# Modulation vectors summed by one matmul after a trip through DRAM

## The reference

```python
c_act = jax.nn.silu(c)                       # c: 1 x 1024
mod = c_act @ ada_w[i] + ada_b[i]            # ada_w[i]: 1024 x 9*1024
sh1, sc1, g1, sh2, sc2, g2, sh3, sc3, g3 = jnp.split(mod, 9, axis=-1)
h = modulate(rms_norm(x, ln_ffn1[i]), sh1, sc1)
x = x + 0.5 * g1[:, None, :] * swiglu(h, ffn1_wg[i], ffn1_wu[i], ffn1_wd[i])
h = modulate(rms_norm(x, ln_mix[i]), sh2, sc2)
...
```

## Time and profile before

| | |
|---|---|
| device time, median of 3 runs | 1738.8 us (1735.62 to 1738.81) |
| span of the profiled execution | 1734.1 us (its own device time is not given) |
| TensorE (PE) busy | 1708.0 us, 98% |
| VectorE (DVE) busy | 1412.9 us, 81% |
| ScalarE (ACT) busy | 908.4 us, 52% |
| POOL busy | 435.0 us, 25% |
| DMA | 411.45 MB, mean 237 GB/s; up to 363 GB/s in F0 |
| steps that add tiles into the accumulator (L2927) | 420, 315.3 us of VectorE |
| loads of modulation tiles by POOL (L2163) | 448 of 256 KB |

### The profile page before, as it was taken

How to read it: one execution, slowest core, us unless ns; L and a number is a source line. 1 busy time by engine, 2 the same in 40 slices (tenths; PEclk the granted TensorE clock), 3 DMA queues, 4 the chain that set the end, 5 groups by cost and what they waited for, 6 DMA issues and landing times. The chain is left out here.

```text
span 1734.1 us, 36503 instructions
## 1 busy us (share of the span) xinstructions
PE 1708.0 (98%) x14039; PEld 1667.7 (96%) x14039; DVE 1412.9 (81%) x1924; ACT 908.4 (52%) x1274; POOL 435.0 (25%) x685
## 2 busy tenths in 40 slices
PE   7999999999999999999999999999999999999998
PEld 5999999999999999999999999999999998799998
DVE  6877898788778977898987799779988896788655
ACT  3443367764335533365634356667444567764444
POOL 6322321012223122321232224540322232401000
PEclk9999999999999999999999999999999999999999
DMA  9998858549887787867698865334988772257550
GB/s 338 356 359 279 294 178 280 166 158 321 304 304 242 276 302 270 302 212 272 229 314 305 302 199 191 115 132 156 322 297 293 230 199 83 78 199 251 184 176 25
DMA packets 261793, 411.45 MB, mean 237 GB/s; under 512 B 21950, under 2 KB 204414, under 8 KB 261560
## 3 DMA queue, kind: packets, MB, share of 16 engines
q1 hardware_dynamic: 224968, 290.67, 51.0%
q0 software_dynamic: 36720, 119.36, 19.4%
HBM read 408.90 MB, written 2.63 MB: 237 GB/s over the span
## 5 line engine op out<-in xcount | busy, mean ns | idle before, releaser
L2891 DVE TENSOR_TENSOR lo<-raw,hi 128x2048 fp32r<-128x2048 f32 (+2 forms) x251 | 565.6, 2256 | 162.4 <-ACT hi L2719 161.8
L2719 ACT CAST hi<-raw 128x2048 fp32r<-128x2048 f32 (+2 forms) x266 | 497.4, 1872 | 377.6 <-PE dacc L2388 189.4
L2386 PE MATMUL up<-operand_hi,hi 128*128 128x256 f32 x1952 | 553.1, 283 | 1.4 <-DVE lo L2891 1.4
L2387 PE MATMUL up<-operand_lo,hi 128*128 128x256 f32 x1952 | 552.3, 283 | 0.0
L2388 PE MATMUL up<-operand_hi,lo 128*128 128x256 f32 x1952 | 552.3, 283 | 0.0
L2163 POOL DMA_DIRECT2D ada<-in_ada_w_dram x448 | 267.3, 613 | 841.8 <-DVE ada_acc L2927 793.5
L2386 PEld LDWEIGHTS up<-operand_hi,hi 128*128 128x128 f32 x1952 | 374.4, 192 | 2.3 <-DVE lo L2891 2.0
L2388 PEld LDWEIGHTS up<-operand_hi,lo 128*128 128x128 f32 x1952 | 374.5, 192 | 0.0
L2387 PEld LDWEIGHTS up<-operand_lo,hi 128*128 128x128 f32 x1952 | 374.5, 192 | 0.0
L2927 DVE SCALAR_TENSOR_TENSOR ada_acc<-ada,c_col,ada_acc 128x512 f32<-128x512 f32 x420 | 315.3, 751 | 13.8 <-DMA ada<-in_ada_w_dram 0.6
L2386 PE MATMUL dacc<-act_hi,hi 128*128 128x256 f32 x976 | 276.2, 283 | 0.7 <-DVE act_lo L3103 0.7
(11 more groups left out here) (483 smaller groups left out, 2858.2 us busy)
## 6 DMA issues: line engine op xcount, KB each, us to landing
ada<-in_ada_w_dram POOLq DMA_DIRECT2D x448, 256.0 KB, 4.8
raw<-in_ffn_wg_dram SPq DMA_DIRECT2D x88, 512.0 KB, 5.4
raw<-in_ffn_wu_dram SPq DMA_DIRECT2D x88, 512.0 KB, 5.2
raw<-in_ffn_wd_dram SPq DMA_DIRECT2D x88, 512.0 KB, 5.6
raw<-in_ffn_w_up_dram SPq DMA_DIRECT2D x88, 512.0 KB, 4.6
raw<-in_ffn_w_down_dram SPq DMA_DIRECT2D x46, 512.0 KB, 4.6
raw<-in_hg_w_in_dram SPq DMA_DIRECT2D x32, 512.0 KB, 4.8
raw<-in_attn_w_qkv_dram SPq DMA_DIRECT2D x24, 512.0 KB, 7.7
```

What stands on the lines that cost most here:

```text
L2386: pe.matmul(o, stat[0], mov[0], start=start, stop=False, skip_group_check=True)
L2387: pe.matmul(o, stat[0], mov[1], start=False, stop=False, skip_group_check=True)
L2719: last = act.copy(put(slab(hi, s, SPL)), take(slab(raw, s, RAW)))
L2891: last = dve.tensor_tensor(put(slab(lo, s, SPL)), take(slab(raw, s, RAW)), put(slab(hi, s, SPL)).bitcast(F32), ALU.subtract)
```

## The change

For v = 2 to 29, with v = 0 and 1 as they were:

- A tile is loaded in one DMA of 512 KB, rows on partitions, and the accumulator is 128 x 1024. VectorE adds a tile in one step instead of two; `c_col` has 16 further columns with `c_act` laid 128 to a column, for which SP loads `c` twice more in another layout at the start. A constant `block_ones` (128 x 8) is made by one reduction.
- POOL writes the finished accumulator to `fold_dram` in DRAM (`fold_start`), in 1024 runs of 128 elements (512 bytes), so that row 16a + r of the DRAM tensor holds the output columns of block a from the eight partitions 8r to 8r + 7, one behind the other; it waits for that, and reads the tensor back as 128 x 1024 (`fold_rest`). VectorE adds the eight partial sums of each row and column in one reduction to `folded`, 128 x 128 (`fold_sum`), and PE sums over partitions with one matmul of `folded` with `block_ones`.
- PE's sums stand later: in the loops behind the columns of iteration 4 instead of 3. Those at the ends of F0, F1, F2, F3, C0 and G go into the next phase (`left_vector`); those of A and C1 stay where they are or move into the last `down`. `mod_vector` moves with them, PE's waits for the vectors too, and G's sum waits for the fourth gelu.
- POOL's loop over four vectors is unrolled, with the two fold steps after the fourth load of the next vector. In other phases `fold_start` is ahead of `pre_add` and `fold_rest` behind it. In H and N, POOL waits for the fold's sum before it builds masks and tables, whose place the fold is read into.

```diff
         def tile_steps(m):
 
-            return AG * (m if m < 2 * KB else m - PE_TILES)
+            return AG * m if m < 2 * KB else AG * (2 * KB - PE_TILES) + m - 2 * KB
...
             source = ada_source(v, k) if source is None else source
+            if v >= 2:
+                eng.dma_start(ada_place(m), source).then_inc(full, 16)
+                return
             for j in range(AG):
...
             for r0, name in ((0, "c"), (ASTEPS, "c_2")):
                 sp.dma_start(c_rows[r0:r0 + ASTEPS, 0:AQ],
-                             T[name].rearrange("b (i q) -> (b i) q", q=AQ)).then_inc(S["c_in"], 16)
+                             T[name].rearrange("b (i q) -> (b i) q", q=AQ)).then_inc(S["lam_in"], 16)
+                sp.dma_start(c_wide[2 * ASTEPS + r0 // AG:2 * ASTEPS + r0 // AG + KB, :],
+                             T[name].rearrange("b (k p) -> (b k) p", p=P)).then_inc(S["lam_in"], 16)
...
+            def fold_start(v):
+
+                pool.wait_ge(S["ada_step"], tile_steps(tile_index(v, KB - 1) + 1))
+                if v > 2:
+                    pool.wait_ge(S["folds"], 16 * FOLDS * (v - 2))
+                pool.dma_start(fold_dram.rearrange("(a r) (g j) -> (r g) a j", a=KB, g=KB),
+                               ada_acc.rearrange("p (a j) -> p a j", a=KB)).then_inc(S["folds"], 16)
+
+            def fold_rest(v):
+
+                pool.wait_ge(S["folds"], 16 * FOLDS * (v - 2) + 16)
+                if v > 2:
+                    pool.wait_ge(S["fold_summed"], v - 2)
+                if v == FIRST_VEC["A"]:
+                    pool.wait_ge(S["qk_logits"], HEADS)
+                pool.dma_start(fold_place(v), fold_dram).then_inc(S["folds"], 16)
...
+                    if left_vector(p) is not None:
+                        fold_start(left_vector(p))
                     pre_add(p)
+                    if left_vector(p) is not None:
+                        fold_rest(left_vector(p))
...
-                        with pool.Fori(0, (FI - 3) // 2) as it:
+                        for u in range(v, v + 4):
                             for k in range(KB):
-                                ada_load(pool, v + 1, k, it, w[u // n][k * P:(k + 1) * P, bass.ds(it * D + (u % n) * D, D)])
+                                if k == ATILES:
+                                    fold_start(u)
+                                    fold_rest(u)
+                                ada_load(pool, u + 1, k)
...
             def ada_sum(v, it=0, o=bank(misc, 1)):
 
-                pe.wait_ge(S["ada_step"], tile_steps(tile_index(v, KB - 1) + 1) + ASTEPS * it)
                 if v >= 2:
+                    pe.wait_ge(S["fold_summed"], v - 1 + it)
                     pe.wait_ge(S["mod_done"], v + it)
+                    pe.matmul(o[:, 0:KB], folded[:, :], block_ones[:, :], start=True, stop=True,
+                              skip_group_check=True).then_inc(S["ada_summed"], 1)
+                    return
...
                 down(0, start=True)
                 ups(2)
+                if left_vector(p) is not None:
+                    ada_sum(left_vector(p))
                 down(1)
                 with pe.Fori(0, (FI - 3) // 2) as it:
                     for i in (3, 4):
                         ups(i, it)
-                        if p in five_vectors and i == 3:
+                        if p in five_vectors and i == 4:
                             ada_sum(v, it)
                         down(i - 1, it)
-                if v is not None and p not in five_vectors:
-                    ada_sum(v)
-                down(FI - 1, stop=True)
-                if p in five_vectors:
-                    ada_sum(v + 4)
+                alone = v is not None and p not in five_vectors
+                down(FI - 1, stop=True, between=(lambda: ada_sum(v)) if alone else None)
...
             def ada_tile(v, k, it=0):
...
+                if v >= 2:
+                    c = c_col[:, 2 * ASTEPS + (KB if v >= V2 else 0) + k:2 * ASTEPS + (KB if v >= V2 else 0) + k + 1]
+                    if k == 0:
+                        dve.wait_ge(S["ada_summed"], 2)
+                        if v > 2:
+                            dve.wait_ge(S["folds"], 16 * FOLDS * (v - 3) + 16 + 16 * FOLDS * it)
+                        dve.tensor_scalar(ada_acc[:, :], ada_place(m), c, None, ALU.mult).then_inc(S["ada_step"], 1)
+                        return
+                    dve.wait_ge(S["ada_step"], tile_steps(m) + KB * it)
+                    dve.scalar_tensor_tensor(ada_acc[:, :], ada_place(m), c, ada_acc[:, :],
+                                             ALU.mult, ALU.add).then_inc(S["ada_step"], 1)
+                    return
...
+            def fold_sum(v, it=0):
+
+                dve.wait_ge(S["folds"], 16 * FOLDS * (v - 1) + 16 * FOLDS * it)
+                dve.wait_ge(S["ada_summed"], v + it)
+                dve.tensor_reduce(folded[:, :], fold_place(v).rearrange("p (g j) -> p j g", g=KB), AX,
+                                  ALU.add).then_inc(S["fold_summed"], 1)
...
                 iteration(1, 0, v, 0, (0, 2, 2), ahead=p in raw_first)
-                iteration(2, 0, v, 4, (2, 1, 1))
+                if left_vector(p) is not None:
+                    fold_sum(left_vector(p))
+                iteration(2, 0, v, 4, (2, 1, 1), summed=left_vector(p))
...
-                    iteration(3, it, v + 1 if more else None, 0, (0, 0, 4), summed=v if more else None)
+                    iteration(3, it, v + 1 if more else None, 0, (0, 0, 4), folding=v if more else None)
...
-                    iteration(4, it, v + 1 if more else None, 4, (2, 0, 2) if conv else (1, 1, 2))
+                    iteration(4, it, v + 1 if more else None, 4, (2, 0, 2) if conv else (1, 1, 2), summed=v if more else None)
...
                 if v is not None and not more:
+                    fold_sum(v)
                     mod_vector(v)
```

More of the change, by code:

```diff
@@ L52 @@
 ASTEPS = KB * AG
+C_ROWS = 2 * ASTEPS + 2 * KB
+FOLDS = 2
 PE_TILES = KB // 2
@@ L1002, in pe_gating @@
                 col_product(b + 6 + m, bank(up, m))
+            pe.wait_ge(S["gelu_done"], 4)
+            ada_sum(left_vector("G"), o=bank(dacc, 0))
             pe.wait_ge(S["ws_done"], 1)
@@ L1123, in dve_gating @@
             split_lo_half(b + 8, 1)
+            mod_vector(left_vector("G"), psum=bank(dacc, 0))
             gate(0)
@@ L1817, in pe_nsa @@
             compressed_scores()
+            ada_sum(left_vector("N"), o=bank(dacc, 3)[:, SEQ:SEQ + KB])
             pe.wait_ge(S["w1_in"], 64)
@@ L2028, in dve_nsa @@
             split_lo(b + 8)
+            mod_vector(left_vector("N"), psum=bank(dacc, 3)[:, SEQ:SEQ + KB])
             query_rest(3)
@@ L2595, in ups, with down @@
                         col_product(s, bank(up, j), p if (i, j) == (1 if p in raw_first else 0, 0) else None)
-                def down(i, it=0, start=False, stop=False):
+                def down(i, it=0, start=False, stop=False, between=None):
                     s = b + (3 * i + 4 if i < FI - 1 else FFN_SLABS - 1)
@@ L2865, in _ @@
             act.wait_ge(S["start_pe"], 1)
-            act.activation(c_col[:, :], bank(misc, 0)[:, 0:2 * ASTEPS], ACT.Silu).then_inc(S["start_act"], 1)
+            act.activation(c_col[:, :], bank(misc, 0)[:, 0:C_ROWS], ACT.Silu).then_inc(S["start_act"], 1)
             for c in range(4):
@@ L2914, in ada_tile @@
                 full, count = tile_full(m)
[L2915 to L2917 removed]
+                dve.wait_ge(full, count + 32 * it)
+                if v >= 2:
[10 more added lines that the diff above has]
+                    return
                 acc = acc_of(v)
@@ L3104, in hidden_lo, with iteration @@
                                       ALU.subtract).then_inc(S["actlo_done"], 1)
-                def iteration(i, it=0, vec=None, k0=0, count=(0, 2, 2), summed=None, ahead=False):
+                def iteration(i, it=0, vec=None, k0=0, count=(0, 2, 2), summed=None, folding=None, ahead=False):
                     a = b + 3 * i - 1
@@ L3123, in iteration @@
                     hidden_lo(i, it)
+                    if folding is not None:
+                        fold_sum(folding, it)
                     if summed is not None:
@@ L3163, in _ @@
             link(dve.tensor_reduce(group_ones[:, :], ident.rearrange("p (q g) -> p g q", g=AG), AX, ALU.add))
+            link(dve.tensor_reduce(block_ones[:, :], ident.rearrange("p (a r) -> p a r", a=KB), AX, ALU.add))
             dve.wait_ge(S["start_act"], 1)
```

84 lines of the change are left out of this document (49 added, 35 removed).

## The result

The kernel before takes 1738.3 us (median of 4 runs, 1735.62 to 1738.81), the changed one 1747.12 us (median of 4, 1745.33 to 1749.59): a ratio of 1.0054, 95% interval 1.0042 to 1.0066. I had forecast 1723.0. The profiled execution of the changed kernel took 1749.59 us for a span of 1747.9, so 1.7 us lie around a span; that of before, with 1734.1, was then near the fastest of its runs.

What follows compares the result with a forecast made beforehand. TensorE, busy 98% of the span, was taken as the bound. Terms −15.0 + 1.3 − 1.8 − 1.1 − .5 + .9 + .4 = −15.8 on the span of 1734.1, plus 4.7 around it, gave 1723.0 us, range 1716 to 1733.

Steps and rivals of the forecast that it cites:

- Price of a sum: TensorE's sums inside the product stream: .21 to .22 us instead of .89, saving .68 at 22 places, −15.0 us.
- Rival (a): The short sum costs what four passes cost, so 22 sums save .45 instead of .68; 1729 us, chance .09.
- Moved sums and the phase ends: Six sums moved into next phases cost +1.3 us; five phase transitions give −.36 each, −1.8; G's end into F3, −1.1.
- Inside C0's end: PE waits .75 us for act_lo behind a VectorE chain with two tiles; forecast to give −.5 us.
- The start: Two more DMAs on SP ahead of x and the first modulation weights: +.9 us, bounds 0 and 1.2.
- VectorE's bill: Per vector −1.8 us on tiles and a reduction of about 1.2; +.4 us allowed where PE soon needs VectorE.
- The allowance of .4: +.4 us for VectorE's new steps in A, H, N and ahead of G's gate, bounds 0 and 3.
- The trip to DRAM: POOL's write and read back of the fold takes 12 to 17 us, decides nothing below some 20 us: 0 us.
- Rival (c): Trip longer than some 20 us in the loops, each us over costing PE one in 20 rounds; 1763 us, chance .08.
- (b): Full DMA engines of F0 and F1 push slabs back, two or three folds at up to 2.9 us; 1729 to 1731, chance .06.
- (d): The write's issue takes 4.8 us and delays pre-adds by 2 us at six phase starts; 1735 us, chance .05.
- What lies around the span: Time of the whole run outside the profiled span, taken as 4.7 us, the median 1738.8 against the span 1734.1.

Runs made afterwards that it cites:

- run 3: Changed kernel with the reduction moved behind the four tiles of iteration 3 in all loops; 1722.8 us, ratio .9916 against the kernel before.
- run 5: Changed kernel with the reduction behind the four tiles in C0's loop alone; 1733.3 us, ratio .9975 against the kernel before.
- run 6: Changed kernel with two tiles ahead of the reduction and two behind it, in all loops; 1727.5 us, ratio .9935 against the kernel before.
- run 9: Changed kernel with reduction behind tiles as three additions, write ahead of fourth tile load, added c loads on ACT, C1's fold summed ahead of its loop; 1729.5 us.
- run 11: Changed kernel with reduction behind tiles as three additions, write ahead of fourth tile load, added c loads on ACT; 1720.5 us, ratio .9901.

## Why the prediction was wrong

- **Price of a sum: right.** .23 us instead of .89 in the trace, .67 gained in 21 of the 22 places, −14.1 for the −15.0 forecast. The 22nd, in A, gave nothing, since TensorE waits for VectorE behind it. Rival (a) falls.
- **Moved sums and the phase ends: right where VectorE is in time.** In run 3 a transition gives −.5 to −.9 (forecast −.36), and −1.8 into F3 (forecast −1.1); the moved sums cost .2. Inside C0's end nothing came of the −.5: the wait of .75 us at act_lo is still .69. In the changed kernel the same ends cost +.4 to +2.4, since VectorE comes to them late: TensorE's five waits for act_lo, 8.0 us.
- **The start: right**, +1.0 for +.9.
- **VectorE's bill: mis-sized.** The 1024-wide step is 1.28 us (forecast 1.30) and the first one, a plain multiplication, .74. The reduction takes 2.03 us, not 1.2: the earlier trace rows have sums of neighbours, and I carried them to a reduction with a stride of 512 bytes without giving it a bound. The allowance of .4 was too small for A alone: .4 us of waiting at the sum, then products at .21 for more than 3 us (the clock .57 between 259 and 262.8 us), 2.3 us in all. In run 5, where the clock stays at full level there, TensorE waits 1.03 us at L507 a little later instead, and A still costs 1.9 us more than before.
- **The trip to DRAM: here it failed.** This is the step of the prediction that failed: "the trip decides nothing below some 20 us: 0 us". The duration was nearly right, 12 to 17 us forecast and 15.1 to 18.5 measured in 18 of the 20 loop rounds (C0's and F0's the longest; 13.2 and 12.8 in the first rounds of F1 and F2, where VectorE did not wait). Wrong was the point from which it decides. I set the trip against one place of F0, where the old kernel's VectorE has 15.4 us and then 5 us of lead, and called everything below 20 us free. But VectorE's tiles stand behind the wait and the next tile 7 behind them; the lead is spent once, and in the next round the trip starts later. The right sum is that of the ring: 34.8 − 19.6 = 15.2 us in the F phases (14.8 in F2) and 34.8 − 21.7 = 13.1 in C0. Those 18 trips were at or above it, in C0 by 2.0 to 5.4 us. And I had looked at F0 only; C0 has the taps in the same series, 2 us more. What it cost is the difference to run 3, 24 us for a term that was put at 0. Rival (c) named the mechanism, with .08, and a price of 20 us for each us, but from the wrong point.
- **The low clock was no term.** The two waits of 3.3 and 3.0 us in C0 cost 5.8 us each. A wait of TensorE had been priced at its length.
- **Rivals (b) and (d)**: F0's and F1's loops gained their 2.7 us with the DMA engines at a share of 1.01 to 1.03 up to 133 us and .91 to .92 from there and in F1, so no slab was pushed back. The write's issue took .91 us, not 4.8, and no pre-add was late.
- **What lies around the span** is 1.7 us, not 4.7. The forecast had taken the distance from the span of one fast run to the median of others for it.

The sum of the prediction without its main error is run 3: the same work, the reduction 4.6 us later in its round, and 1722.8 us where 1723.0 was forecast. That it fits to .2 us is luck: its span is 1720.8 where about 1718 was forecast, which the 4.7 us for 1.7 made good, and within the span the transitions gave about 2 us more than forecast, while A, N and the time behind the last slab cost some 4 us more.

## What to carry to other kernels

Before a round trip (DRAM, another engine) goes into a loop whose engines run in fixed order, add up the ring: the trip and everything that stands in series behind the wait for it, up to the instruction that starts the next trip, in each loop that holds it, and compare with the period of the bounding engine. A lead that one round shows is spent only once. When the ring is too long, do not shorten the trip first; move work that doesn't need it from behind the wait to ahead of it: that cost nothing here and was worth 24 us. And price a wait of TensorE of some 3 us above its length: nine waits of 2.4 to 4.8 us in these traces made their slab end .5 to 2.8 us later than their length alone would.

## What the runs showed of the hardware

- Each of the ten waits of TensorE of 2.3 to 4.8 us behind the start was followed by 2.9 to 6.0 us at a granted clock of .50, products .21 us apart. Behind shorter ones it fell in some places (1.84 us at 747.5 in the changed kernel, 1.25 at 831.2 in the kernel before) and not in others (2.07 us at 1021.9 in the changed one). A wait does not decide alone: in A, at the sum, the clock fell in most traces that have the wait of .38 us there, but not in runs 5 and 6, and it fell in runs 9 and 11, which have no such wait; in N no wait over .35 us stands within 10 us ahead of it.
- A VectorE reduction of 1024 fp32 elements to 128 takes 1.22 us over neighbours and 2.03 us over elements 512 bytes apart. Three additions of 512, 256 and 128 elements take .68, .45 and .29 us.
- A 512 KB write to DRAM in 1024 runs of 512 bytes is issued by POOL in .91 us and lands 3.8 us after the start of its issue at best, 8.7 by the median with two or three 512 KB loads of the same queue still under way, and 6.1 in the loops with none of them. A 512 KB load of whole rows is issued in .53 us.
- Beside two copies of POOL of .62 us each an 8-column step of VectorE took 1.53 us instead of .17.
